# A hybrid decoder step on one core: parameter rows laid out by feature, the order at the joints of the mix blocks, and the last feed-forward turn

## What is computed

```python
n = rms_norm(x, g_mix)
q, k, v, xr, gr, gates = jnp.split(n @ w_in, SPLITS, axis=-1)
attn = attend(q, k, v, sb_bias)          # stick-breaking weights: exp(log_sigmoid(z) + suffix sum)
xc, rnn_buf_new = causal_dwconv(xr, rnn_buf, w_rnn_conv, b_rnn_conv)       # 4 taps
hseq, h_last = rg_lru(xc, rnn_h0, w_rgate, b_rgate, w_igate, b_igate, rglru_lambda)
rnn = hseq * jax.nn.gelu(gr)
gate_a, gate_b = jnp.split(jax.nn.sigmoid(gates), 2, axis=-1)
x = x + (gate_a * attn + gate_b * rnn) @ w_out
up, ffn_buf_new = causal_dwconv(rms_norm(x, g_ffn) @ w_up, ffn_buf, w_ffn_conv, b_ffn_conv)  # 3 taps
ua, ub = jnp.split(up, 2, axis=-1)
x = x + (jax.nn.gelu(ua) * ub) @ w_down
y = rms_norm(x, g_final)
```

## Time and profile before

| what | value |
|---|---|
| median of three runs | 1985.5 us (1978.39 to 1987.98) |
| the profiled execution's own time | 1983.88 us |
| its span | 1982.1 us |
| mean granted clock of PE | 0.968 of full |
| PE busy | 1844.0 us (93%) |
| PE weight loads busy | 1718.3 us (87%) |
| DVE busy | 1193.6 us (60%) |
| ACT busy | 908.0 us (46%) |
| POOL busy | 192.2 us (10%) |
| one addition to y (`add_down`, L2074), mean of 240 | 514 ns |
| one step of `score_out` (L1048), mean of 136 | 697 ns |
| one scan (L1167), mean of 136 | 1258 ns |

### The profile page before, as it was taken

One profiled execution on the slowest core, in us unless ns is written; L12 is line 12 of the kernel. 1 busy time (PEld: TensorE's weight loads), 2 busy tenths in 40 slices (PEclk: granted clock), 3 DMA queues, 4 the chain that ended last, 5 costly groups with the idle time before them and its releaser, 6 DMA issues. The chain is left out here.

```text
span 1982.1 us, 39881 instructions
## 1 busy us (share of the span) xinstructions
PE 1844.0 (93%) x14474; PEld 1718.3 (87%) x14474; DVE 1193.6 (60%) x2001; ACT 908.0 (46%) x1483; POOL 192.2 (10%) x96
## 2 busy tenths in 40 slices
PE   6899799999999999999997999999999999999987
PEld 5898787878787879787786999999999999999976
DVE  6100476858595868777686355665466556656644
ACT  5111567676867676676766343122122112211223
POOL 0111000000000000000000002222122112212210
PEclk9999899999999999999998999999999999999989
DMA  4356313132322322141312311211111111111102
GB/s 138 105 153 149 104 40 107 46 113 58 89 69 85 87 68 81 50 117 35 104 35 89 131 31 37 61 53 42 35 55 55 37 42 53 53 32 53 53 22 92
DMA packets 212173, 141.45 MB, mean 71 GB/s; under 512 B 56127, under 2 KB 203712, under 8 KB 212000
## 3 DMA queue, kind: packets, MB, share of 16 engines
q1 hardware_dynamic: 212026, 139.58, 24.2%
HBM read 120.16 MB, written 19.62 MB: 71 GB/s over the span
## 5 line engine op out<-in xcount | busy, mean ns | idle before, releaser
L87 PE MATMUL t_banks<-n_hi,d_w_hi 128*128 128x344 f32 (+1 forms) x1056 | 338.2, 320 | 3.5 <-ACT d_up L1789 2.0
L87 PE MATMUL t_banks<-n_hi,d_w_lo 128*128 128x344 f32 (+1 forms) x1056 | 338.5, 321 | 0.0
L87 PE MATMUL t_banks<-n_lo,d_w_hi 128*128 128x344 f32 (+1 forms) x1056 | 337.7, 320 | 0.0
L87 PE MATMUL b_p_proj<-n_hi,b_w_hi 128*128 128x350 f32 x768 | 266.3, 347 | 15.0 <-DVE b_w_lo L1133 13.1
L2074 DVE TENSOR_TENSOR mix<-mix,t_banks 128x344 f32<-128x344 f32 (+1 forms) x240 | 123.4, 514 | 251.8 <-PE t_banks L2197 251.8
L87 PE MATMUL b_p_proj<-n_lo,b_w_hi 128*128 128x350 f32 x768 | 253.2, 330 | 0.0
L87 PE MATMUL b_p_proj<-n_hi,b_w_lo 128*128 128x350 f32 x768 | 252.5, 329 | 0.0
L1744 POOL TENSOR_TENSOR d_w_lo<-w_raw,d_w_hi 128x1024 fp32r<-128x1024 f32 x45 | 108.9, 2421 | 1411.5 <-ACT d_w_hi L1774 1411.5
L1789 ACT ACTIVATE d_up<-t_banks 128x344 f32<-128x344 f32 (+1 forms) x126 | 57.3, 455 | 372.2 <-PE t_banks L87 372.1
L87 PEld LDWEIGHTS t_banks<-n_hi,d_w_hi 128*128 128x128 f32 x1056 | 199.2, 189 | 4.5 <-ACT d_up L1789 2.6
L87 PEld LDWEIGHTS t_banks<-n_lo,d_w_hi 128*128 128x128 f32 x1056 | 198.7, 188 | 0.0
(11 more groups left out here) (264 smaller groups left out, 3790.1 us busy)
## 6 DMA issues: line engine op xcount, KB each, us to landing
w_raw<-in_w_in SPq DMA_DIRECT2D x45, 512.0 KB, 4.4
w_raw<-in_w_up SPq DMA_DIRECT2D x45, 512.0 KB, 3.9
b_page<-in_cache_k SPq DMA_DIRECT2D x128, 128.0 KB, 2.1
b_page<-in_cache_v SPq DMA_DIRECT2D x128, 128.0 KB, 2.1
w_raw<-in_w_down SPq DMA_DIRECT2D x22, 512.0 KB, 3.5
b_q_in<-q_scr SPq DMA_DIRECT2D x128, 64.0 KB, 2.0
mix<-in_x_prompt SPq DMA_DIRECT2D x8, 512.0 KB, 6.9
q_scr<-r_rg SPq DMA_DIRECT2D x16, 256.0 KB, 3.5
```

The costliest lines, as they stand in the source:

```text
L87: last = pe.matmul(out, w[:, k, :], x[:, k, col:col + width], start=(k == 0 and w is w_hi and x is x_hi), stop=(k == KT - 1 and w is w_lo))
```

## The change

The diff has five parts.

1. The host lays out both sets of parameter rows by feature, so `par` and `fpar` are filled by one DMA each; the transposes, DVE copies and buffers of the rows go. The kept states leave the core by feature too, `kept_x` and `kept_h` before the feed-forward loop and `kept_u` after the last convolution, and the host puts them back into rows. The 60 transposes, 15 ACT copies and six DMAs for them go.
2. In `phase_mix` PE issues the scores of a block's first slot at the end of the last slot of the block before (for the first block ahead of everything).
3. ACT does `act_gates` after the copies, Exp and Ln of slot 0.
4. In slot 9 DVE copies the turned weights before `positive` and `summing`.
5. The last turn of DVE's feed-forward loop is written out: the last convolution is interleaved with the eight additions, four of them behind it, and a_hi and a_lo of the last turn are made by chunk of columns. PE waits for the a_lo of its chunk, no longer for all.

```diff
-                for r, n, src in ((R_CONVSTATE, 24, g.state_rnn_conv.rearrange("o s j d -> (o s j) d")),
-                                  (R_H0, 8, g.state_rnn_h[0]), (R_CONVW, 4, g.w_rnn_conv[0]),
-                                  (R_CONVB, 1, g.b_rnn_conv), (R_BR, 1, g.b_rgate), (R_BI, 1, g.b_igate),
-                                  (R_LAM, 1, g.rglru_lambda), (R_GMIX, 1, g.g_mix), (R_GFFN, 1, g.g_ffn)):
-                    sp.dma_start(rows[r:r + n, :], src).then_inc(rows_in, 16)
+                sp.dma_start(g.par[:, :, :], g.par_mix).then_inc(rows_in, 16)
...
                     if t == 1:
-                        dve.wait_ge(rows_t, 1)
-                        dve.tensor_copy(g.par[:, :, :].rearrange("p k r -> p (k r)"),
-                                        pt[:, 0:KT * N_ROWS]).then_inc(params, 1)
-                        dve.wait_ge(params, 1)
+                        dve.wait_ge(rows_in, 16)
...
                         if s == 0 and not first:
                             weights(i, -2)
-                            act.wait_ge(proj_out, nth(i, CHUNK_NS, -1, 2))
-                            branch.act_gates(act, i - 1)
                         score_out(i, s, first)
...
                         act.activation(so, so, ACT.Ln, bias=1.0).then_inc(soft_done, 1)
+                        if s == 0 and not first:
+                            act.wait_ge(proj_out, nth(i, CHUNK_NS, -1, 2))
+                            branch.act_gates(act, i - 1)
...
+                        if s == 9:
+                            for n in range(min(groups, 2)):
+                                turn_out(i, v, n)
                         if u >= 0 or not first:
                             positive(i, u)
                             summing(i, u)
-                        for n in range(min(groups, 2)):
-                            turn_out(i, v, n)
+                        if s != 9:
+                            for n in range(min(groups, 2)):
+                                turn_out(i, v, n)
...
-                        if s == 0:
-                            scores(i, 0)
                         decode(i, s, first)
                         if s + 1 < SLOTS:
                             scores(i, s + 1)
-
+                        elif i + 1 < KT:
+                            scores(i + 1, 0)
+
+                scores(0, 0)
                 slots(0, True)
...
+                sp.dma_start(fpar[:, :, :], g.par_ffn).then_inc(par_arr, 16)
+                for to, rows in ((g.kept_x, g.x_out), (g.kept_h, g.h_out)):
+                    sp.dma_start(to, rows[:, :, :]).then_inc(rows_stored, 16)
...
+                sp.wait_ge(conv_done, 2 + 4 * TURNS)
+                sp.dma_start(g.kept_u, g.u_out[:, :, :]).then_inc(rows_stored, 16)
...
                 act.wait_ge(down_done, DOWNC * TURNS)
-                for n in range(FPAIR):
-                    high_a(TURNS - 1, n)
+                for c in range(CHUNKS):
+                    c0, width = LCH[c]
+                    for n in range(FPAIR):
+                        act.wait_ge(prod_done, nth(TURNS - 1, FPAIR, n, 2))
+                        act.activation(a_hi[:, n, c0:c0 + width], prod[:, n, c0:c0 + width],
+                                       ACT.Copy).then_inc(a_hi_ready, 1)
...
+                    if between[0]:
+                        add_down(i - 1, between[0])
                     own.step(dve.scalar_tensor_tensor(c[:, FTOK:LAST], x[:, FTOK - 1:LAST - 1], cw(1),
                                                       c[:, FTOK:LAST], ALU.mult, ALU.add))
+                    if between[1]:
+                        add_down(i - 1, between[1])
...
+                        part = down_part(u)
+                        if last and u == 3:
+                            conv(m + 1, u, None, (part[0:2], part[2:4]))
+                        else:
+                            add_down(m, part)
+                            conv(m + 1, u)
...
+                with dve.Fori(0, TURNS - 2, 1) as m:
+                    up_turn(m, False)
+                up_turn(TURNS - 2, True)
+                for c in range(CHUNKS):
+                    c0, width = LCH[c]
+                    if c == 0:
+                        add_down(TURNS - 2, down_part(3)[4:5])
+                    for n in range(FPAIR):
+                        dve.wait_ge(a_hi_ready, FPAIR * (TURNS - 1) + FPAIR * c + n + 1)
+                        dve.tensor_tensor(a_lo[:, n, c0:c0 + width], prod[:, n, c0:c0 + width],
+                                          a_hi[:, n, c0:c0 + width].bitcast(F32), ALU.subtract).then_inc(a_lo_ready, 1)
+                    if c == 0:
+                        add_down(TURNS - 2, down_part(3)[5:8])
...
-                    if n == 4:
-                        params()
...
-                pe.wait_ge(a_lo_ready, FPAIR * TURNS)
-                pe.wait_ge(conv_done, 2 + 4 * TURNS)
                 for c in range(CHUNKS):
                     c0, width = LCH[c]
+                    pe.wait_ge(a_lo_ready, FPAIR * (TURNS - 1) + FPAIR * (c + 1))
...
-                        if c == 0:
-                            for r in range(2 * tile, min(2 * tile + 2, len(kept))):
-                                rows(r)
```

More of the change, by code:

```diff
@@ L478, in _ @@
                     last.then_inc(x_turned, 1)
-                    if t == 0:
-                        pe.wait_ge(rows_in, 16 * 9)
-                        for k in range(KT):
-                            last = pe.transpose(pt[:, N_ROWS * k:N_ROWS * (k + 1)], rows[:, P * k:P * (k + 1)],
-                                                g.ident[0:N_ROWS, 0:N_ROWS])
-                        last.then_inc(rows_t, 1)
                     if t in (5, 7):
@@ L2086, in _, with up_turn @@
                         gated(0, u // 2)
[L2087 removed]
+                def up_turn(m, last):
                     own.turn(4 * CONV, m, 4 * CONV)
@@ L2234, in _ @@
                         down(m, nth(m, 6, 7, 2), down_part(u))
-                def rows(n):
-                    src, first, to = kept[n]
-                    if n >= 2:
-                        pe.wait_ge(rows_out, n - 1)
-                    for r in range(4):
-                        last = pe.transpose(p_par[0:to.shape[0], n % 2, P * r:P * (r + 1)], src[:, first + r, :],
-                                            g.ident[:, :])
-                    last.then_inc(rows_turned, 1)
                 def turn_y(t):
```

127 lines of the change are left out of this document (42 added, 85 removed).

## The result

| | before | after |
|---|---|---|
| median | 1983.7 us (4 runs beside after's) | 1966.3 us (1961.73 to 1967.99, 4 runs) |
| ratio, 95% interval | 1 | 0.9907 [0.9888, 0.9926] |
| span of the profiled execution | 1982.1 us | 1965.8 us |
| mean granted clock of PE | 0.968 | 0.973 |

The change gives 17.4 us in the medians and 16.3 us in the spans, where 35.3 were forecast, and 1966.3 lies just above the range. The busy times of the page of the profile have hardly moved. First the list of PE's waits in the changed kernel (line and releaser, then us in total, times, longest); the earlier trace rows and the 9.34 us of the earlier trace rows are what it answers to.

What follows compares the result with a forecast made beforehand. PE, 93% busy, was taken as the bound, so only its idle time and clock could be won back. Terms of 18.0 + 2.5 + 1.9 + 1.0 + 2.9 + 9.0 = 35.3 us off 1985.5 gave 1950.2 us, range 1937 to 1965.

Steps and rivals of the forecast that it cites:

- order at the seven joints: Scores moved ahead of the block joints and gates behind: 27.1 - 6.1 (k_in waits) - 3 (clock) = 18.0 us gained.
- first block: Scores ahead of all projections, so the 1.8 us stall and 0.9 us of scores go: 2.5 us, bounds 1.0 and 2.9.
- tenth slot: Slot 9's w_t wait of 2.4 us goes; nothing gained by itself, only clock: 1.9 us, bounds 0 and 3.8.
- start: Parameter rows come in one load, without transposes and a DVE copy: 1.0 us, bounds 0 and 1.3.
- parameters of the feed-forward: 44 transposes leave PE's chain and 18 loads become one: 2.9 us, bounds 2.0 to 4.9.
- last turn: Last down projection starts 2.5 us earlier and 60 transposes go for 6.5: 9.0 us, bounds 8.0 and 14.4.
- the term of 27.1 us: Seven joints' distances from the second slot's copy end to the third slot's scores, 3.2 to 4.7 us each, booked as gain.
- rival (a): The clock falls at every joint and tenth slot: 10.5 us lost instead of 3, no 1.9; 1959.6 us, chance 0.17.
- the term of 1.6 us for a_hi and a_lo of one chunk: In the last turn, a_hi and a_lo of some 40% of the columns take 1.6 us before PE starts.
- Slower rival: Rival (c): DVE's wait for later gates is uncovered, each joint costs 3.1 us; about 1990 us, chance 0.05.
- signs of being right: At joints: no score wait of 4 us or more, seven of about 1 to 3, ACT without a gap.
- rival (b): The tenth slot's stall is simply gone, seven times 2.4 instead of 1.9: 1935 us; chance 0.13 with larger gains.

Runs made afterwards that it cites:

- e6: The kernel before with 62 idle PE products in each joint ahead of the second slot's scores: 1973.1 us, ratio 0.9944.
- e2: The kernel before with only the scores moved (part 2), gates still ahead of the first slot's copy: 1982.4 us, ratio 0.9984.
- e8: The kernel before with the tenth slot's new order (part 4) alone: 1984.3 us, ratio 1.0006.
- e10: The kernel before with 62 idle products in each joint and 34 ahead of slot 9's value products: 1967.4 us, ratio 0.9923.
- e12: The changed kernel with DVE's last turn in the old order, additions then convolution, a_hi and a_lo still by chunk: 1968.1 us, ratio 0.9927.
- e16: The changed kernel unaltered, run and traced again: 1967.3 us, ratio 0.9925.
- e9: The changed kernel with part 4 undone, 40 idle products ahead of the third slot's scores and 34 ahead of slot 9's value products: 1950.3 us, ratio 0.9830.

## Why the prediction was wrong

| step | forecast, us | traces, us |
|---|---|---|
| order at the seven joints | 18.0 | 3.2 |
| first block | 2.5 | 3.3 |
| tenth slot | 1.9 | -7.0 |
| start | 1.0 | 2.35 |
| parameters of the feed-forward | 2.9 | 2.4 |
| last turn | 9.0 | 10.4 |
| end of the mix phase | 0 | 1.7 |
| together | 35.3 | 16.3 |

**Joints: the step that failed is the term of 27.1 us, and the 3 us beside it.** The distances from copy to scores did go, from 27.1 to 0.7 us. But 14.6 of them (27.1 - 12.5) were work at half clock behind the old stall, as e6 shows by taking the clock's fall alone away. The forecast booked them as won, and charged the new stall of 2.9 us with two falls of 1.5 us at most likely. The new stall made the clock fall in all seven, one slot later: between the third and the fourth slot's scores the lead shrinks by 13.9 us in all, 2.0 a joint. The text had even said that the distance "exceeds 3.2 where the clock was low", and then left it in the sum. The waits for k_in were forecast at 6.1 us and are 7.0, to which one of 1.7 for q_in comes in the last joint. 26.4 - 13.9 - 8.7 = 3.8 against 3.2 measured. The rival (a) had the mechanism and too small a price: 1.5 for each fall, against 2.0.

**Why the stall was longer than forecast** (2.9 us, not 1.2 to 2.3): from the start of the second slot's scores PE needs 5.65 us to the third's at full clock (307.04 to 312.69, where the wait begins), and 7.0 us in the kernel before, behind its stall (315.48 to 322.46). The forecast carried the second over. It is the same mistake once more.

**Tenth slot.** That the edit gives nothing by itself held to 0.15 us a block. The step that failed is "what it can give is the clock": the forecast let it only rise, since one stall of 2.4 us went. The waits of 1.4, 0.5 and 1.3 us let it fall as well, in the first block behind the last of them and in the fifth to eighth behind the one of 0.5. These falls are dearer: in the kernel before four of the six are half as long as the other two and cost 0.1 to 0.2, since PE's wait for r_gr half a slot later, 0.95 us in the second block, is gone behind them; the two long ones cost 1.5. In the changed one four are long and cost 1.8 to 2.2, and the first block's is short but has no such wait behind it and costs 1.5. The bound of 0 from below was wrong. Rival (a) had a fall in every tenth slot, but only as a gain of 1.9 that does not come, not as a loss.

**Start.** More than the bound of 1.3: DVE's first multiplication by the gain starts at 10.20 instead of 12.09, 1.9 us earlier and not 1.1, and PE's first piece at 26.72 instead of 28.35. The rows behind it come 2.35 us sooner. The x tiles' loads, no longer behind nine others, were put down as a condition and not as a gain; that they are the rest is argued, not shown.

**First block, parameters.** The first block gave 3.3 us, above its bound of 2.9; e2 has it alone (the second slot's scores 3.4 us sooner). The parameters gave 2.4 us for the 2.9 taken, inside their bounds: PE's first waits in the feed-forward move from 1228.5 and 1244.7 to 1222.3 and 1238.8, with a lead of 5.9 to 6.2 where the last scores of the mix had 1.9 and w_out's wait 3.6. The 1.7 us between those last two are no effect of the change: in this trace of the kernel before the clock falls behind a wait of 1.7 us for a cache page at the end of the phase, and the traces of e8 and e10, with the old order behind the last scores, have no fall there.

**Last turn.** Nearly right in size, and right on the two collisions with POOL and on PE's wait in the last down groups, 3.6 us. The start came 1.4 us sooner for the 2.5 taken. The collisions took 4.2 us, less than the 4.7 put down for them; what was too small is the term of 1.6 us for a_hi and a_lo of one chunk. From `d_prod` to the product it is 3.1 us: ACT waits for PE's last down groups, and one addition stands ahead of a_lo. The forecast had seen those groups held up, but called it "inside the same time". The transposes gave their 6.5: from the start of the last product to the end it is 55.6 us before and 49.1 in e12, which starts at 0.50 as well. The rest, about 2 us, is clock that the forecast did not see: the old product began at 0.50 after a stall of 9.3 us, the new one at 1.00. That part is not sure of an execution: in e16 the clock falls just behind the product's start, and the turn's gain is 8.6 us instead of 10.4.

**Slower rival.** DVE's gate wait was covered: DVE waits 3.0 us for the gate activations (its `gate` starts at 307.53, just after ACT is done with the second) and again 3.25 us for ACT before its step at 317.82, and PE has no wait for DVE in between. Wrong in one more point: the text offered "a joint gain of less than 2 us" as the sign of DVE being late. The mean gain is 0.5 us, and DVE was not the cause. The signs of being right that the text listed for the joints (seven waits of 1 to 3 us, ACT without a gap) nearly all came true with a sixth of the gain, for none of them looked at the clock.

**Sums.** Three do not come out as written: six times 0.6 is 3.6 and not 3.8, rival (b) is 14.9 below and not 15.1, and the last turn's bounds, 8.0 and 14.4, are not those of its parts, 2.0 and 6.7 with the 6.5, which give 8.5 and 13.2. None of them changes the outcome.

## What to carry to other kernels

A gap read from a trace holds the clock of that trace: before a wait is booked as a gain, look at the granted clock in the stretch behind it, and scale PE's work there to full clock. Here a stall that was cut from 4.4 to 2.9 us still cost a fall in each of the seven joints, and a fall cost least where PE had a wait behind it that could shrink. A trace is one execution: the same kernel's tenth stretches took 207.2 and 201.1 us in two. Fill the wait that stays with other work, and with idle products to learn what it is worth: that is one small experiment, and here it told more than the change itself.

## What the runs showed of the hardware

- A run of 62 products of 128 columns in 3.64 us (59 ns each), with PE otherwise waiting, kept the granted clock at 1.00 from 310 to 322 us; without them it was 0.50 from 316 to 318.
- PE's clock fell behind a single wait of 2.9 us in all seven joints, and in some blocks, not in others, behind the waits of 1.4, 0.5 and 1.3 us of the tenth slot. With the waits over 2 us filled (e9), the tenth stretches of seven blocks agree within 0.03 us (24.71 to 24.74); with the waits left, the same order gives 24.75 to 26.26 in the kernel before.
- A pair of DVE steps of 8 columns took 2.74 us and one step of 1026 columns 2.79 us while POOL subtracted, 0.49 and 0.81 when it did not (the changed kernel and e12). The additions to y, which read PSUM, kept their 0.51 us under POOL in e12.
